# Alternating the matmul passes of two output tiles between their two PSUM banks in a decoder trunk

## What is computed

```python
for layer in range(DEPTH):
    if layer < N_A_LAYERS:      # layer 0: convolution module
        ...                     # x @ pw1 (1024 to 2048), gate, 31-tap depthwise conv, layer norm, silu, @ pw2
    else:                       # layer 1: differential attention
        ...                     # q, k, v projections, two softmaxes per head, output projection w_o
    x = conv_ffn(x, ...)

def conv_ffn(x, norm_g, w_in, dw_w, dw_b, w_out):
    h = rms_norm(x, norm_g)
    u = causal_depthwise_conv(h @ w_in, dw_w, dw_b)          # w_in: 1024 x 5632, three taps
    gate, up = u[..., :D_FF], u[..., D_FF:]                  # D_FF = 2816
    return x + (jax.nn.silu(gate) * up) @ w_out              # w_out: 2816 x 1024
```

## Time and profile before

| | us |
|---|---|
| median of 3 runs | 1284.3 |
| lowest, highest | 1284.09, 1289.94 |
| profiled execution | 1283.49 |
| its span, first to last instruction | 1281.7 |

### The profile page before, as it was taken

How to read it: one execution, slowest core, us unless ns; L and a number is a source line. 1 busy time by engine, 2 the same in 40 slices (tenths; PEclk the granted TensorE clock), 3 DMA queues, 4 the chain that set the end, 5 groups by cost and what they waited for, 6 DMA issues and landing times.

```text
span 1281.7 us, 16583 instructions
## 1 busy us (share of the span) xinstructions
PE 1238.3 (97%) x6085; PEld 1021.3 (80%) x6085; DVE 843.0 (66%) x1158; ACT 544.3 (42%) x942; POOL 111.2 (9%) x99
## 2 busy tenths in 40 slices
PE   6998997999999999999999999997999999999999
PEld 4787756788888888887998889966888888888887
DVE  7999946577627763676577777665577537762673
ACT  6256955444314431345454545433444324431441
POOL 4000001200000000002324141401200000000000
PEclk9999998999999999999999999998999999999999
DMA  5221001222322222223221212211222322232222
GB/s 212 81 91 59 1 5 53 98 76 98 109 89 98 98 99 99 81 74 109 96 70 34 67 34 67 66 33 33 99 94 91 111 69 96 98 118 79 99 74 91
DMA packets 16615, 104.00 MB, mean 81 GB/s; under 512 B 1840, under 2 KB 1968, under 8 KB 5424
## 3 DMA queue, kind: packets, MB, share of 16 engines
q1 hardware_dynamic: 16560, 103.25, 24.2%
HBM read 101.15 MB, written 2.10 MB: 81 GB/s over the span
## 4 chain that ended last, share of the span: by engine, by line
PE 89%; DVE 6%; ACT 3%; POOL 1%; issue 1%; DMA 0%; SPq 0%; POOLq 0%; DVEq 0%; ACTq 0%
PE bank L1034 67%; PE bank L1152 9%; PE bank L1088 5%; PE bank L1184 2%; PE bank L1214 2%; POOL sq_sum L415 1%; DVE w_lo L707 1%; DVE w_lo L699 1%; ACT prob L661 1%; DVE prob L980 1%; PE bank L1105 1%; PE bank L1187 1%; DVE prob L982 1%; PE bank L1079 1%; DMA w_raw<-stream 0%
## 5 line engine op out<-in xcount | busy, mean ns | idle before, releaser
L1034 PE MATMUL bank<-xg_hi,w_hi 128*128 128x512 f32 x832 | 326.8, 393 | 13.6 <-DVE xg_lo L715 11.1
L1034 PE MATMUL bank<-xg_lo,w_hi 128*128 128x512 f32 x832 | 325.0, 391 | 0.0
L1034 PE MATMUL bank<-xg_hi,w_lo 128*128 128x512 f32 x832 | 325.0, 391 | 0.0
L470 ACT ACTIVATE w_hi<-w_raw 128x2048 fp32r<-128x2048 f32 x83 | 158.3, 1907 | 156.5 <-PE bank L1034 156.5
L699 DVE TENSOR_TENSOR w_lo<-w_raw,w_hi 128x2048 fp32r<-128x2048 f32 x83 | 192.6, 2320 | 30.9 <-ACT w_hi L470 30.9
L1034 PE MATMUL bank<-act_hi,w_hi 128*128 128x512 f32 x480 | 193.2, 402 | 8.9 <-DVE act_lo L831 7.2
L1034 PEld LDWEIGHTS bank<-xg_hi,w_hi 128*128 128x128 f32 x832 | 156.9, 189 | 48.3 <-DVE w_lo L730 11.1
L1034 PE MATMUL bank<-act_lo,w_hi 128*128 128x512 f32 x480 | 190.8, 398 | 0.0
L1034 PE MATMUL bank<-act_hi,w_lo 128*128 128x512 f32 x480 | 190.6, 397 | 0.0
L604 ACT ACTIVATE ffn_t<-ffn_u,par 128x512 f32<-128x512 f32 x88 | 72.0, 818 | 268.6 <-DVE ffn_u L884 268.6
L1034 PEld LDWEIGHTS bank<-xg_lo,w_hi 128*128 128x128 f32 x832 | 157.0, 189 | 33.3 <-issue 0.7
(11 more groups left out here) (141 smaller groups left out, 1607.6 us busy)
## 6 DMA issues: line engine op xcount, KB each, us to landing
w_raw<-stream SPq DMA_DIRECT2D x87, 1024.0 KB, 4.9
w_raw<-stream SPq DMA_DIRECT2D x8, 768.0 KB, 4.3
x<-x_t SPq DMA_DIRECT2D x8, 256.0 KB, 6.8
out_t<-x SPq DMA_DIRECT2D x8, 256.0 KB, 2.0
w_raw<-stream SPq DMA_DIRECT2D x2, 512.0 KB, 5.1
par<-params SPq DMA_DIRECT2D x1, 345.5 KB, 2.9
lam_in<-lambdas SPq DMA_DIRECT2D x1, 128.0 KB, 8.6
```

The costliest lines, as they stand in the source:

```text
L470: act.activation(w_hi[:, j, :], w_raw[:, j, :], ACT.Copy).then_inc(w_hi_done, 1)
L1034: got = pe.matmul(out, weights(w, j, k, m), v[:, k, :], start=(k == 0 and s == 0), stop=(k == count - 1 and s == 2), skip_group_check=True)
```

## The change

In `unit`, a first loop now takes the input tiles but the last two (or but the `late` ones, where these are more). For each input tile it issues the three kinds of pass in turn, and each kind for both output tiles before the next: six passes that go to bank 2j, 2j + 1, 2j, 2j + 1, and so on. The last two input tiles are taken as before, tile by tile. `between`, where it falls in this part, now comes behind all six passes of its input tile. The passes, their weights and the order of sums within a bank are the same, and so are the programs of all other engines. The lines below it move down by ten, so L1063 is L1073 afterwards, and the alternating passes have line L1053.

```diff
--- before.py
+++ after.py
@@ -1044,7 +1044,17 @@
 
                 begin(n)
                 early = count - late
-                order = [(m, k) for m in range(2) for k in range(early)]
+                both = min(early, count - 2)
+                for k in range(both):
+                    if ready:
+                        ready(k)
+                    for s, (w, v) in enumerate(((w_hi, hi), (w_hi, lo), (w_lo, hi))):
+                        for m in range(2):
+                            pe.matmul(bank[2 * j + m][:, :], weights(w, j, k, m), v[:, k, :], start=(k == 0 and s == 0),
+                                      stop=False, skip_group_check=True)
+                    if between and k == at:
+                        between()
+                order = [(m, k) for m in range(2) for k in range(both, early)]
                 if late <= 2:
                     order += [(m, k) for m in range(2) for k in range(early, count)]
                 else:
```

## The result

| | before | after |
|---|---|---|
| median us | 1287.12 (4 runs) | 1388.58 (4 runs) |
| lowest, highest | 1284.09, 1291.57 | 1384.70, 1388.97 |
| profiled execution, its span | 1283.49, 1281.7 | 1388.60, 1386.7 |
| mean granted clock in it | 0.991 | 0.980 |

The ratio is 1.0778, 95% interval 1.0735 to 1.0822: slower by nearly 8%. The forecast was 1380.5, with 1362 to 1408 as the range. The three runs of before that the forecast started from had a median of 1284.3; a fourth moved it to 1287.12. Between the medians lie 101.5 us, where 96.2 were forecast.

What follows compares the result with a forecast made beforehand. TensorE, busy 97% of the span and 89% of the last chain, was taken to bound the kernel. Terms of 79.4, 9.4, 2.8, 2.2 and 2.4 gave 96.2 us, added to the 1284.3 median: 1380.5 us, range 1362 to 1408.

Steps and rivals of the forecast that it cites:

- Passes cost what they did: TensorE's 2808 alternating passes: changing banks was taken to alter the time per pass by 0.
- The chain through VectorE: Each unit: first tile complete at pass 42, eviction, weight split, next unit; 12.77 us instead of 10.88, 1.89 more.
- (1): Feed-forward input units: 42 waits for the weight split behind tile 0's eviction, 1.89 us each, 79.4 us.
- (2): First projection: units 2 to 6 delay units 3 to 7, 5 x 1.89 = 9.4 us.
- term (3): End of the first projection: the convolution's first group waits longer for the last tile's low part, 2.8 us.
- term (4): First feed-forward unit of each layer: later sum of squares makes the reciprocal late, 1.1 us, twice 2.2.
- term (5): Output units of six input tiles: the last input tile is ready late, 1.2 us, twice 2.4.
- Rival (a), the clock: TensorE's clock falls in the new waits: all falling 75 us, one in three 26 us, 1406 us; chance 12%.
- Nothing for attention: Attention stage: no added time, 0 us, since its passes are untouched.

Runs made afterwards that it cites:

- late_first: Changed kernel without alternation: six input tiles go to the second tile, then the first, which still finishes with pass 42; 1385.98 us, ratio 1.0793.
- by_input: Changed kernel, but in the first six input tiles the bank changes after every third pass; first tile still finished with pass 42; 1387.16 us, ratio 1.0793.
- a_repair: Changed kernel's TensorE program, with VectorE's split of the next unit's weights moved ahead of the first tile's eviction; 1302.76 us, ratio 1.0134.
- b_again: The kernel before, unchanged, profiled once more; 1291.15 us for the profiled execution.
- alt5: Changed kernel with alternation in the first five input tiles only, first tile finished with pass 39; 1349.89 us, ratio 1.0523.
- alt3: Changed kernel with alternation in the first three input tiles only, first tile finished with pass 33; 1292.83 us, ratio 1.0042.
- alt4: Changed kernel with alternation in the first four input tiles only, first tile finished with pass 36; 1314.80 us, ratio 1.0262.
- b_repair: The kernel before, TensorE's order kept, with VectorE's weight split moved ahead of the first tile's eviction; 1290.18 us, ratio 1.0028.

## Why the prediction was right

**Passes cost what they did.** A unit of the kernel after that has no wait ahead of it, with 36 alternating passes, first and last pass:

```profile
271.20 0.62 PE L1053 MATMUL bank<-xg_hi,w_hi 128*128 128x512 f32 x2
...
281.85 0.39 PE L1034 MATMUL bank<-xg_hi,w_lo 128*128 128x512 f32 x1
```

Forty-seven distances in 10.65 us are 0.2266 us each, and 0.2267 was the reading of the earlier trace rows. (x2 stands for two passes in a row in one entry, here one for each bank.) The passes on `act_hi` and `act_lo`, 0.2333 us apart in the earlier trace rows, kept their distance too: 20 alternating ones from 632.50 to 637.17 are 0.2335 each. The test that the trace of before offered in the earlier trace rows, bank changes after every third pass, had told it rightly, and `late_first` and `by_input` confirm it from the side of the total. The Trainium skill (TensorE: Matmul & The Clock Gate, "Back-to-back issue gap") gives 216 ns as the gap of isolated matmuls of 512 columns, and 131 ns for a stream of them with their weight loads; the prediction named only the first, and called it that of a stream. Passes with a weight load each took 227 ns here, above both, and with either order of the banks, so the 11 ns to the first do not come from the bank, and the second was not met.

**The chain through VectorE.** Forecast 1.89 us a unit, measured 12.80 - 10.88 = 1.92, each link within 0.02. Terms (1) and (2), forecast 88.8 us, are 47 x 1.92 = 90.2. The three kernels with fewer tiles test the same chain at other points; those with four and five lie within 2 us of their forecasts, the one with three is told above.

**The end of the first projection**, term (3), forecast 2.8. VectorE's two evictions and the convolution's wait, which answer to the earlier trace rows:

```profile
114.70 0.69 DVE L793 TENSOR_TENSOR conv_a<-bank,rs 128x512 f32<-128x512 f32 x1 [1.63 <-PE bank L1034]
...
118.83 0.68 DVE L798 TENSOR_TENSOR conv_a<-bank,rs 128x512 f32<-128x512 f32 x1
...
123.48 0.79 PE L1098 MATMUL bank<-u_hi,diag 128*128 128x512 f32 x1 [6.07 <-DVE u_lo L810]
```

The evictions are 4.13 us apart, as summed, and the wait is 6.07 where it was 3.31: 2.76 more. The stage lost 3.5; behind the longer wait the granted clock stayed at 0.50 for 6.8 us instead of 3.4 (121.2 to 128.1), which the sum had left out and which costs 0.7 to 0.8.

**The late reciprocal**, term (4), forecast 1.1 a layer. It answers to the earlier trace rows:

```profile
269.36 3.35 DVE L741 RECIPROCAL rs<-ms 128x512 f32<-128x512 f32 x1 [2.72 <-ACT ms L495]
272.74 0.69 DVE L884 TENSOR_TENSOR ffn_u<-bank,rs 128x512 f32<-128x512 f32 x1
...
281.58 0.68 DVE L884 TENSOR_TENSOR ffn_u<-bank,rs 128x512 f32<-128x512 f32 x1
```

The unit after it started 13.31 us after its forerunner (271.20 to 284.51), 0.65 more than the 12.66 of the chain. The term was too large by 0.45. Some 0.3 of that is in a second condition before the change: ScalarE's root (L495) started at 251.75, behind a table load that ended at 251.63, although the matmul of the squares had ended at 251.44. So the 18 passes of delay did not all reach the reciprocal.

**The output units of six tiles**, term (5), forecast 1.2 each:

```profile
639.44 0.50 PE L1034 MATMUL bank<-act_hi,w_hi 128*128 128x512 f32 x1 [0.94 <-DVE act_lo L900]
```

0.94 us idle and the slow second pass make 1.05, and by the next unit's start it is 1.2.

**Rival (a), the clock.** Forty-five waits of 1.62 to 1.63 us left the clock where it was, and so did the 45 each in the traces of `by_input` and `late_first`. The other two of the 47, 2.27 us long and behind the late reciprocal, parted: in layer 0 the clock fell, in layer 1 it did not.

```profile
284.51 0.77 PE L1053 MATMUL bank<-xg_hi,w_hi 128*128 128x512 f32 x2 [2.27 <-DVE w_lo L699]
...
285.10:288.40 3.30, 3.30 (x9) 2.62 (x8) 2.13 (x5) 1.64 (x3) 0.00 (x0) 0.50 0.87 285
...
1002.62 0.73 PE L1053 MATMUL bank<-xg_hi,w_hi 128*128 128x512 f32 x2 [2.27 <-DVE w_lo L699]
1003.19 0.63 PE L1053 MATMUL bank<-xg_lo,w_hi 128*128 128x512 f32 x2
```

The passes behind the first take 0.43 us each at 0.50 of the clock; behind the second they are at full pace. That fall is the 1.6 us by which feed-forward 0 lost more than feed-forward 1. The prediction held its waits of 1.6 us to be safe because a fall stood behind 2.44 us and none behind 2.25. The waits were safe, but there is no such bound. The traces of all the kernels, with the longest of the short waits in TensorE's queue:

| idle us | where | clock fell to 0.50 | stayed at 1.00 |
|---|---|---|---|
| 3.24, 3.27 | low part of the product, six-tile output units | `a_repair`, layer 1 | `a_repair`, layer 0 |
| 2.41 to 2.44 | before unit 2 of the first projection | before, `b_again`, after, `by_input`, `alt5` | `late_first`, `alt3`, `alt4` |
| 2.27 | second unit of feed-forward 0 | after, `by_input`, `late_first` | |
| 2.27 | second unit of feed-forward 1 | | after, `by_input`, `late_first` |
| 2.24 to 2.26 | attention, L1171 in before | `b_again`, after, `by_input`, `late_first`, `alt3` | before, `alt4`, `alt5`, `a_repair` |
| 1.81, 1.84 | before unit 2 of the first projection | `b_repair` | `a_repair` |
| 1.62, 1.63 | the new waits | | 45 each in after, `by_input`, `late_first` |

Two of these rows, first `late_first`, then `b_repair` (the wait, then a window behind it with its granted clock):

```profile
40.15 0.50 PE L1034 MATMUL bank<-xg_hi,w_hi 128*128 128x512 f32 x1 [2.41 <-DVE w_lo L699]
...
40.20:44.20 4.00, 4.00 (x18) 3.27 (x19) 4.00 (x7) 0.82 (x2) 0.00 (x0) 1.00 0.75 244
```

```profile
38.22 0.54 PE L1039 MATMUL bank<-xg_hi,w_hi 128*128 128x512 f32 x1 [1.84 <-DVE w_lo L699]
...
38.50:41.90 3.40, 3.40 (x9) 2.66 (x9) 3.40 (x6) 0.00 (x0) 0.00 (x0) 0.51 0.77 248
```

The clock fell behind 1.84 us once and held behind 3.24 once, and behind 2.25 us it did both in one and the same program. So the length of a wait alone does not decide, and what does was not tested. With waits somewhat longer than these 1.6 us, the two rows would have been no ground for a forecast of the up to 75 us of rival (a).

What the Trainium skill tells of banks in rotation (TensorE: Matmul & The Clock Gate, "A second HAM failure mode: psum-queue depth-cycling") did not show here: the idle between groups was 1.63 us and the clock held behind it, and where it fell behind a wait of 2.27 us it fell in `late_first` too, where the banks hardly change.

**What the sum left out.** 105.0 was measured between the spans and 96.2 forecast: 8.8 us. Attention has 5.9 of them, which goes with the granted clock; the clock behind the reciprocal 1.6, behind the convolution's wait 0.7; 1.2 in small pieces less the 0.6 of the earlier start make up the rest. Set side by side at about equal mean clock, the difference is nearer to the forecast: the runs after have a median of 1388.6 (three of the four at 0.980), the four of before at 0.980 and 0.981 a mean of 1291.0, 97.6 apart. The step that was off is the prediction's "Nothing for attention", together with the first profile, at 0.991, taken as typical of both kernels; the stage measured 5.9 us more, and a spread from 1284.1 to 1289.9 in the three runs shown gave a hint that a stage had two lengths. That the result lies in the range in spite of it is in this part luck: the range's width stood for other terms.

## What to carry to other kernels

When two accumulations are interleaved, ask when the first of them is finished, and what stands behind its consumer in that engine's queue. Here nothing depended on the order of the banks; but work for the *next* unit stood behind the first tile's eviction, and there was room for nine more passes ahead of that tile's end (24 to 33) before the next unit had to wait, ten by the sum, and 0.23 us a unit for every pass beyond. A chain of a few links read from one stretch of the trace (last pass to eviction, eviction to split, split to first pass) gave the length of a unit here to within 0.03 us. And before a few microseconds are given to a change, compare runs at equal mean granted clock.

## What the runs showed of the hardware

Passes of 128 x 512 with a weight load each start 0.2266 us apart whether the bank changes after every pass or only after 24 (0.2333 to 0.2335 for those on `act`, in both cases). The first pass after a wait at full clock is followed by its second 0.34 us later. The mean granted clock in attention was 0.98 or 0.95 in two executions of one program, and 6.9 us of the stage's length went with it. A wait of 2.25 us in TensorE's queue did or did not lower the clock in two executions of one program; over all traces it fell once behind 1.84 us and held once behind 3.24 us; behind 1.62 to 1.63 us it held in all 135 cases.
